# Attention: half of the scores' second pass on half of the array's rows, all turned blocks copied by ScalarE, and the squares of the attended rows on GpSimd

## What is computed

```python
def one_block(qblk):
    s = jnp.einsum('bqhmd,bkhmd->bhmqk', qblk, k,
                   preferred_element_type=jnp.float32) * ATTN_SCALE
    p = jax.nn.softmax(s, axis=-1)
    a = p[:, :, 0] - lam * p[:, :, 1]
    return jnp.einsum('bhqk,bkhv->bqhv', a.astype(v.dtype), v)
...
ao = (rms_norm(attn_o, subln_g) * (1.0 - lam_init)).reshape(b, n, ATT_WIDTH)
```

## Time and profile before

| | us |
|---|---|
| median of 3 runs | 1809.46 |
| lowest and highest run | 1807.63, 1817.28 |
| profiled execution: span from its first to its last instruction | 1803.4 |
| median less that span | 6.06 |

### The profile page before, as it was taken

The page is one execution under the profiler, slowest core; times in us unless marked ns, Lnnn a source line. Parts: engine busy times, 40 slices in busy tenths (PEclk is TensorE's granted clock), DMA queues, the critical chain, the costliest instruction groups (busy, mean ns, idle before and its releaser), DMA issues.

```text
span 1803.4 us, 22828 instructions
## 1 busy us (share of the span) xinstructions
PE 1742.9 (97%) x8677; PEld 1461.8 (81%) x8677; DVE 1212.7 (67%) x1390; ACT 800.6 (44%) x1253; POOL 759.5 (42%) x450
## 2 busy tenths in 40 slices
PE   6999999989998899999999999999999999999999
PEld 4788887888888688788888889978888888878887
DVE  3734799578898616854545743786666667689865
ACT  3522222667677325533333432754435444444443
POOL 2332422000001142466666520548999999810000
PEclk8999999999999999999999999999999999999999
DMA  9567123000000731222221611303232232286433
GB/s 358 204 216 238 48 83 117 4 24 1 0 0 1 245 106 47 59 82 59 60 81 59 198 59 47 117 24 106 82 93 83 72 92 82 85 329 223 147 122 123
DMA packets 165385, 188.32 MB, mean 104 GB/s; under 512 B 9454, under 2 KB 117543, under 8 KB 165159
## 3 DMA queue, kind: packets, MB, share of 16 engines
q1 hardware_dynamic: 165287, 187.00, 31.7%
HBM read 152.37 MB, written 34.60 MB: 104 GB/s over the span
## 4 chain that ended last, share of the span: by engine, by line
PE 53%; DVE 4%; ACT 2%; issue 1%; DMA 1%; SPq 0%; ACTq 0%; DVEq 0%
PE ps L3217 20%; PE ps L2225 15%; PE ps L3268 10%; PE ps L2285 5%; PE ps L3568 1%; PE ps L3230 1%; DVE cv_lo_p L132 1%; DVE up_lo_p L132 1%; DVE residual L2147 0%; ACT residual L3404 0%; PE ps L3234 0%; DVE residual L3126 0%; DMA w_raw<-in_ffn_w_out 0%; ACT cv_hi_p L129 0%; ACT residual L1964 0%
## 5 line engine op out<-in xcount | busy, mean ns | idle before, releaser
L3217 PE MATMUL ps<-up_hi_p,st_hi_p 128*128 128x512 f32 x560 | 218.7, 391 | 2.9 <-ACT residual L2935 2.9
L3217 PE MATMUL ps<-up_lo_p,st_hi_p 128*128 128x512 f32 x560 | 218.5, 390 | 0.0
L3217 PE MATMUL ps<-up_hi_p,st_lo_p 128*128 128x512 f32 x560 | 218.3, 390 | 0.0
L3268 PE MATMUL ps<-down_ring 128*128 128x512 f32 x924 | 210.9, 390 | 2.8 <-DVE down_ring L132 2.6
L3268 PEld LDWEIGHTS ps<-down_ring 128*128 128x128 f32 x924 | 173.0, 188 | 40.5 <-issue 4.0
L132 POOL TENSOR_TENSOR in_lo<-in_raw,in_hi 128x512 fp32r<-128x512 f32 (+1 forms) x54 | 96.9, 1803 | 215.5 <-ACT in_hi L129 215.5
L2225 PE MATMUL ps<-cv_hi_p,cv_st_hi_p 128*128 128x512 f32 x392 | 153.2, 391 | 2.7 <-ACT residual L1943 2.7
L2225 PE MATMUL ps<-cv_hi_p,cv_st_lo_p 128*128 128x512 f32 x392 | 153.0, 390 | 0.0
L2225 PE MATMUL ps<-cv_lo_p,cv_st_hi_p 128*128 128x512 f32 x392 | 153.0, 390 | 0.0
L2067 DVE TENSOR_TENSOR residual<-ps,residual 128x512 f32<-128x512 f32 x70 | 48.3, 691 | 120.0 <-PE ps L2225 120.0
L132 POOL TENSOR_TENSOR st_lo_p<-up_raw,st_hi_p 128x512 fp32r<-128x512 f32 x68 | 101.7, 1499 | 64.4 <-ACT st_hi_p L129 64.4
(11 more groups left out here) (396 smaller groups left out, 4232.4 us busy)
## 6 DMA issues: line engine op xcount, KB each, us to landing
up_raw<-in_ffn_w_in SPq DMA_DIRECT2D x44, 512.0 KB, 5.0
w_raw<-in_ffn_w_out SPq DMA_DIRECT2D x66, 256.0 KB, 2.8
cv_raw<-in_odd_w_in SPq DMA_DIRECT2D x32, 512.0 KB, 5.5
in_raw<-in_even_w_in SPq DMA_DIRECT2D x48, 256.0 KB, 3.9
y_scratch<-residual SPq DMA_DIRECT2D x22, 512.0 KB, 2.6
ada_raw<-in_ada_w SPq DMA_DIRECT2D x16, 512.0 KB, 9.1
square<-in_ada_w SPq DMA_DIRECT2D x16, 512.0 KB, 4.3
rest_odd<-in_ada_w SPq DMA_DIRECT2D x16, 512.0 KB, 4.4
```

Of the source, the lines that this page charges most:

```text
L3217: last = pe.matmul(ps[:, bank(j, p), :], w[p][:, kk * P:(kk + 1) * P], x[p][:, kk, :], start=(first and w is st_hi and x is up_hi), stop=( ...
L3268: last = pe.matmul(ps[:, 4 * (i % 2) + m, :], slot[:, s, m * P:(m + 1) * P], slot[:, x, :], start=(k == 0 and s == 0 and x == 2 and DOWN[i ...
```

## The change

1. **Scores.** In tiles 2 to 7 the second pass no longer runs all 512-column products over all 128 rows. Of the low part of k only the columns 1024 to 1279 are multiplied as before. Columns 0 to 511 are multiplied with q high on rows 0 to 63 alone, columns 512 to 1023 with q high on rows 64 to 127 alone (`q_upper`), into two banks. For that SP copies the high part of q from partitions 0 to 63 to partitions 64 to 127 once per head and map, from SBUF to SBUF. PE waits for it before tile 2. All first-pass products now stand ahead of the second pass.
2. **Copies.** ScalarE copies all three rounds into `mixed_t`, which has one buffer now. Only the very last tile's round 0 is left to VectorE.
3. **Squares.** For heads 0 to 2 `finish` only scales. GpSimd squares the whole head's rows in one instruction and sums them in seven halving steps (`squared`), behind its copies for the next head. In the last head ScalarE squares as before (`finish_squared`; `SQUARED_BY_POOL` is 0). ScalarE's splits for the output product wait for the sums of head 2.

ScalarE's order in the program of a step within a head, before: rounds 1 and 2, the two exponentials, the scaled copy and the square.

The diff, cut to what matters:

```diff
@@ scalar @@
                             act.wait_ge(sem(f"mix_turned{i}"), n + 1 + (CREDIT if i == LAST else 0))
-                            act.activation(mixed_t[:, t % 2, b * P:e * P],
+                            if i == 0:
+                                act.wait_ge(sem("o_done"), n + CREDIT)
+                            act.activation(turned_mix(h, t)[:, b * P:e * P],
                                            ps[:, i if is_last(h, t) else MIX_BANK, 0:(e - b) * P], ACT.Copy)\
...
-                        def last_rounds(h, t):
-                            for i in range(1, 3):
+                        def rounds_out(h, t):
+                            for i in range(3):
                                 turn_out(h, t, i)
 
                         def tiles(h):
                             for t in range(2, RT):
-                                last_rounds(h, t - 2)
+                                rounds_out(h, t - 2)
                                 for m in range(2):
                                     exps(h, t, m)
                                 if t < L1:
-                                    finish(h, t - 2)
+                                    (finish_squared if isinstance(h, int) and t - 2 >= SQUARED_BY_POOL else finish)(h, t - 2)
                                 if isinstance(h, int) and t - 4 in range(OUT_FIRST):
+                                    act.wait_ge(sem("o_summed"), (HEADS - 1) * SUMS_OF_HEAD + CREDIT)
...
                             tiles(h)
+                            turn_out(h, L2, 0)
                             for m in range(2):
                                 high_k(act, h + 1, m, score[m])
@@ gpsimd @@
+                        def squared(h, end):
+
+                            pool.wait_ge(sem("o_scaled"), h * RT + end + CREDIT)
+                            rows, squares = o_all[:, h, 0:end, :], o_square[:, 0:end, :]
+                            pool.wait_ge(sem("o_summed"), h * SUMS_OF_HEAD + CREDIT)
+                            pool.tensor_tensor(squares, rows, rows, ALU.mult).then_inc(sem("o_summed"), 1)
+                            for i in range(1, SUMS_OF_HEAD):
+                                n = DV >> i
+                                to = squares[:, :, 0:n] if n > 1 else o_stat[:, h, 0:end].unsqueeze(2)
+                                pool.wait_ge(sem("o_summed"), h * SUMS_OF_HEAD + i + CREDIT)
+                                pool.tensor_tensor(to, squares[:, :, 0:n], squares[:, :, n:2 * n], ALU.add)                                    .then_inc(sem("o_summed"), 1)
@@ sync @@
+                        for h in range(HEADS):
+                            for m in range(2):
+                                if h == 0:
+                                    sp.wait_ge(sem("head_high"), m + 1)
+                                else:
+                                    sp.wait_ge(sem(f"scored{m}"), h * RT)
+                                    sp.wait_ge(sem("q_high"), (h - 1) * 2 + m + 1 + CREDIT)
+                                sp.dma_start(q_upper[m][DH:P, :].bitcast(F32), q_turned[0:DH, m, :].bitcast(F32)).then_inc(sem(f"q_raised{m}"), 16)
@@ tensor @@
-                            for b in range(0, KEYS, BANK):
-                                e = min(b + BANK, KEYS)
-                                for part in range(2):
-                                    last = pe.matmul(place(h, t, m)[:, b:e], q_turned[:, m, t * P:(t + 1) * P],
-                                                     k_turned[:, m, part, b:e], start=(part == 0), stop=(part == 1))
+                            tiled = t >= 2
+                            if t == 2:
+                                pe.wait_ge(sem(f"q_raised{m}"), h * 16 + 16)
+                            rows = slice(t * P, (t + 1) * P)
+                            for part in range(2):
+                                for b in range(2 * BANK if tiled and part else 0, KEYS, BANK):
+                                    e = min(b + BANK, KEYS)
+                                    last = pe.matmul(place(h, t, m)[:, b:e], q_turned[:, m, rows], k_turned[:, m, part, b:e],
+                                                     start=(part == 0), stop=(part == 1))
+                            if tiled:
+                                pe.matmul(place(h, t, m)[:, 0:BANK], q_turned[0:DH, m, rows], k_turned[0:DH, m, 1, 0:BANK],
+                                          start=False, stop=True)
+                                last = pe.matmul(place(h, t, m)[:, BANK:2 * BANK], q_upper[m][DH:P, rows],
+                                                 k_turned[DH:P, m, 1, BANK:2 * BANK], start=False, stop=True)
@@ vector @@
                             combine(h1, t1)
                             peaks(h, t, 1)
                             combine_rest(t1)
-                            turn_out(h1, t1)
```

66 lines of the change are left out of this document (42 added, 24 removed).

## The result

| | before | after |
|---|---|---|
| median of the runs, us | 1808.84 (4 runs) | 1830.0 (4 runs) |
| lowest and highest run | 1807.63, 1817.28 | 1821.34, 1831.6 |
| span of the profiled execution | 1803.4 | 1828.5 |

The ratio of the times is 1.0101, 95% interval 1.0079 to 1.0123. The change makes the kernel slower. The predicted direction is right, the predicted time of 1820.0 is 10 us too low, and 1830.0 lies outside the range of 1811 to 1826.

The account below looks back on a forecast made before the run. By busy times TensorE bounds the step, VectorE close behind; after the change a ring of waits through ScalarE was to set it. Terms 3.7 + 1.8 + 2.8 + 0.4 + 1.5 + 0.3 = 10.5 us on 1809.46 gave 1820.0, range 1811 to 1826.

Parts of the forecast that it names:

- steps of heads 0 to 2, ring: Attention, heads 0 to 2, 15 steps t = 3 to 7: each goes from 5.78 to 6.02, 3.7 us more.
- three changes of head with t = 2: Copy 0 on ScalarE stands ahead of the last tile's turn 1: 0.6 us each, 1.8 us more.
- VectorE held up, heads 1 and 2: GpSimd's squares block VectorE's weight operation behind a change of head: about 0.5 us lost per head.
- last head, with its share of the holding up: Squares and output-weight splits stay on ScalarE in the last head: 2.8 us more; GpSimd's blocking 0.5 per head.
- tail: Behind the last head, the last turn 1 waits longer, about half lost in a wait for VectorE's mix: 0.4 us.
- start: Head 0 may wait 0 to 1 us for the copies of q queued on SP behind two loads; 0.3 taken.
- The ring through ScalarE: Attention step: ScalarE's copies and exponentials chained twice through PE set its length, 4.77 + S, 6.02 us.
- S: Time of map 1's scores on PE, up to turn 2: 1.24 us before, put at 1.25 after.
- neither sets the step any more: Attention step: VectorE loses 0.69 and PE up to 0.46 us of work, and both gains turn into idle time.
- No edges: Rival on the scores: half-row pairs run side by side without mode-change cost, S 1.01, 1814.2 us; chance 0.21.
- a pair in a row: Rival on the scores: half-row products run one after another, with edges, S 1.48, 1825.5 us; chance 0.09.
- the sums block the mix each time: Rival: GpSimd's sums hold up VectorE's mix, 2 us more in each of three heads, 1826 us; chance 0.08.

Follow-up runs that it names:

- ring_alone: Changed kernel with GpSimd's copies for the next head back at the change of head and the squares' sums left out; ratio 1.0079 to the kernel before.
- scalar_squares: Changed kernel without GpSimd's squares, ScalarE squaring in all heads as before; 1830.16 us, ratio 1.0101 to the kernel before.
- copies_first: Changed kernel with GpSimd's copies for the next head put ahead of the squares, at the change of head; ratio 1.0101 to the kernel before.

## Why the prediction was too low

| term | predicted | measured in the stage |
|---|---|---|
| steps of heads 0 to 2, ring | 3.7 | 5.9 |
| three changes of head with t = 2 | 1.8 | 1.4 |
| VectorE held up, heads 1 and 2 | 1.0 | 2.6 |
| last head, with its share of the holding up | 2.8 + 0.5 | 3.5 |
| tail | 0.4 | 1.6 |
| start | 0.3 | 1.9 |
| stage | 10.5 | 16.9 |

The ring's 5.9 is head 0 (30.94 - 29.10) and twice `ring_alone` less before (36.93 - 34.88); the 2.6 is twice the rest of a head (38.22 - 36.93). The predicted 3.7 is for t = 3 to 7 alone, with t = 2 in the term below it; the measured 5.9 and 1.4 cut otherwise, with t = 2 of heads 1 and 2 in the 5.9. The two sums, 5.5 and 7.3, compare.

- **The ring through ScalarE** is right, and so is what it makes of the others: PE waits 0.51 before turn 1, released by ScalarE's copy, there is no wait for peaks of map 0, and VectorE has over 0.5 to spare. The step was put at 6.02 and is 6.155 on the mean of 6.05 and 6.26. Two sizes are off. S is 1.30 instead of 1.25. And the step that failed is "neither sets the step any more", said of VectorE and PE: a second ring, over two steps and through map 0's scores, peak 0, the mix and peak 1, comes last once in two steps and adds 0.21 there, 0.10 on the mean. In the 15 steps the 0.135 a step is 2.0 us.
- **The half-row pair** runs side by side, and the mode has edges. Both pages of the Trainium skill that the prediction cites for it are borne out, "TensorE: Matmul & The Clock Gate", Part 3, by the starts, and "TensorEngine Tiling (Array Packing)", Tiling Modes, by the edges. The four full products ahead of the pair take 0.87 (512.28 to 513.15), and 1536 of 2560 columns at the pace of the kernel before would be 0.74. The pair takes 0.43, where one product of 512 columns has 0.25 by that pace. So the edges cost 0.13 and 0.18, not 0.12 each, and S grew by 0.06 instead of 0.01. "No edges" and "a pair in a row" both fall.
- **The change of head** is right to half a microsecond in three.
- **GpSimd** was the rival "the sums block the mix each time" in part. GpSimd's work on the squares takes 0.89 a head instead of 0.5, and by another instruction than the one predicted: the product of 1024 elements took 1.89, not 2.36, and was over when VectorE asked for its weight; it is the first sums that hold the mix for 0.9 (1.65 for 0.75). The step that failed is the sentence that GpSimd's copies stand behind the sums "with five steps of room": they had room for themselves and took it from VectorE, 0.40 a head more. Asked was when their result is needed, not what they hold up while they run. Their length, 2.45 and 2.03 us a pair, and VectorE's mixing were in the trace; that a copy with one input blocks too wasn't, since in the kernel before they ran at the change of head.
- **The last head** at 41.66 is 0.2 above what was predicted, 41.0 and 0.5 for GpSimd's squares. `scalar_squares`, without those, has 40.90, and they add 0.76. The square, put at 0.46 here, is 0.35 of the chain. The second profile's 42.73 has the fall of the clock in it.
- **The tail and the start**: the steps that they contain were judged at the full clock. At the start PE waits 1.32 for the DMA where it waited 0.51 for ScalarE before, so the DMA's share is 0.8, inside the bounds of 0 to 1; then it has half the clock for longer than in the first profile before. In the tail the clock fell in two of three profiles. A clock that falls was in no term, and in the kernel before too it differs from one profile to the next.
- **The last 3.6 us** are outside the stage. The median was put 6.06 above the span, as if that distance were fixed. It isn't: these profiled runs are 1.6 and 1.8 us above their own spans (1830.1 and 1828.5, 1813.36 and 1811.6). The rest of the 6.06 was that the profiled run of the kernel before was a short one. After: the parts outside the stage are 8.2 us longer than in that profile, and the distance 4.6 less. So 10.0 = 6.4 in the stage + 8.2 - 4.6.

Open stays why the clock falls in some runs and not in others, at the start, in the last head, in the tail and outside the stage, and what is left of the start's 1.9 behind the DMA's 0.8 and the clock's 0.5 or so.

## What to carry to other kernels

A ring of waits read off the trace gave direction and mechanism where the busy shares pointed the other way; but look for a second ring about as long as the first, through the engine that seems to have room. It may close only after two steps, and then long and short steps can come by turns, as here. When work moves on an idle engine, cost it twice: whether its result comes in time, and whom it holds up while it runs; moved copies count as much as new work. And take a term per run from two profiles, not from one: here the same code differed by 8 us between two runs, nearly half of what the change did, and one fall of the clock in the last head of `copies_first` took 1.1 us, more than the 0.8 that it had gained in heads 1 and 2. Compare steps with the granted clock beside them.

## What the runs showed of the hardware

- Two products of 512 columns on 64 rows each, into two banks, start within 0.01 us of each other and the pair takes 0.43, the time of one and 0.18 more; with the edge ahead of them the pair gains nothing: 1.30 against 1.24 for the six products.
- A copy by GpSimd, with one input, holds VectorE's two-input mix up like a sum does: 1.69 for 0.75 us. The Trainium skill, "SBUF — State Buffer", section "SBUF: two separate sides", gives the shared port pair to whichever starts first, a VectorE operation with two inputs in SBUF or a GpSimd one that reads SBUF, for the whole instruction. The trace agrees both ways: VectorE's weight took 1.19 for 0.22 behind a sum, and GpSimd's sum of 8 elements took 0.97 for 0.20 beside a mix. VectorE's peaks, with their input in PSUM, were 1.47 to 1.49 in every run.
- ScalarE's square of 128 columns with its sum takes 0.35 of a chain in which nothing waits.
- Two runs of one program had granted clocks of 1.00 and 0.88 in the same 20 us, with PE busy throughout.
